# Between the experts and the next feed-forward: projecting the unnormalised sum

## The reference

```python
# end of first_block: a mixture of 16 experts is added, then a norm
x = x + scatter_add(ye)                       # the sum, 256 x 1024
x = rmsnorm(x, g_final)                       # x * rsqrt(mean(x*x) + 1e-6) * g_final
# start of second_block, for l in 0, 1:
x = x + 0.5 * swiglu(rms_norm(x, norm_ffn1[l]), ffn1_wi[l], ffn1_wo[l])
# swiglu: gate, up = split(x @ w_in); (silu(gate) * up) @ w_out,  w_in 1024 x 5632, w_out 2816 x 1024
```

## Time and profile before

| | us |
|---|---|
| median of three runs | 2795.94 |
| lowest and highest of them | 2792.14, 2796.29 |
| the profiled execution | 2791.85 |
| its span, first to last instruction | 2789.7 |
| first matmul of the first dense slot after the experts | 1437.53 |

### The profile page before, as it was taken

The page is one execution under the profiler, slowest core; times in us unless marked ns, Lnnn a source line. Parts: engine busy times, 40 slices in busy tenths (PEclk is TensorE's granted clock), DMA queues, the critical chain, the costliest instruction groups (busy, mean ns, idle before and its releaser), DMA issues.

```text
span 2789.7 us, 43821 instructions
## 1 busy us (share of the span) xinstructions
PE 2397.6 (86%) x18612; PEld 1867.8 (67%) x18612; DVE 1169.5 (42%) x1679; ACT 840.4 (30%) x1196; POOL 112.7 (4%) x107
## 2 busy tenths in 40 slices
PE   6899988778777877777779997889999999698999
PEld 6896485333333333322259996789999999488999
DVE  6757552100000000000045567566556556755655
ACT  3384121100000000000034444344445444434543
POOL 0000012000000000000010001000001000200000
PEclk9999998887887888888889997899999999699999
DMA  6435047999999999999965541143555554022553
GB/s 226 147 126 175 16 192 281 424 425 426 425 425 425 424 425 425 425 426 425 425 256 187 184 163 61 37 147 123 184 187 195 182 182 159 1 93 97 177 185 117
DMA packets 118618, 669.80 MB, mean 240 GB/s; under 512 B 10682, under 2 KB 12901, under 8 KB 60992
## 3 DMA queue, kind: packets, MB, share of 16 engines
q1 hardware_dynamic: 113376, 650.14, 59.7%
q0 software_dynamic: 2784, 13.21, 1.4%
q10 hardware_dynamic: 2304, 4.20, 0.4%
HBM read 662.26 MB, written 5.24 MB: 239 GB/s over the span
## 4 chain that ended last, share of the span: by engine, by line
PE 54%; DMA 19%; DVE 8%; SPq 7%; issue 3%; ACT 3%; DVEq 3%; POOLq 1%; POOL 0%; ACTq 0%; PEldq 0%; PEld 0%
PE psd L565 29%; PE psx L565 8%; DMA ring<-in_w_up 8%; SPq L2429 7%; DMA ring<-in_w_down 3%; DMA hx<-in_w_down 3%; PE psd L825 3%; DVE w_lo L1642 2%; DMA e_w_lo<-in_w_gate 2%; DMA ring<-in_w_gate 2%; PE psd L816 2%; DVE scr L1642 1%; PE psx L867 1%; PE psx L1062 1%; PE psd L853 1%
## 5 line engine op out<-in xcount | busy, mean ns | idle before, releaser
L565 PE MATMUL psd<-h_hi,w_hi 128*128 128x256 f32 x2448 | 703.2, 287 | 35.0 <-DVE h_lo L1642 12.8
L1642 DVE TENSOR_TENSOR w_lo<-ring,w_hi 128x1024 fp32r<-128x1024 f32 x436 | 524.2, 1243 | 434.7 <-ACT w_hi L1266 432.1
L565 PE MATMUL psd<-h_lo,w_hi 128*128 128x256 f32 x2448 | 697.0, 285 | 0.0
L565 PE MATMUL psd<-h_hi,w_lo 128*128 128x256 f32 x2448 | 696.5, 285 | 0.0
L1266 ACT ACTIVATE w_hi<-ring 128x1024 fp32r<-128x1024 f32 x436 | 435.8, 1047 | 301.6 <-PE psd L565 296.5
L565 PEld LDWEIGHTS psd<-h_hi,w_hi 128*128 128x128 f32 x2448 | 474.1, 194 | 40.9 <-issue 30.8
L565 PEld LDWEIGHTS psd<-h_lo,w_hi 128*128 128x128 f32 x2448 | 474.3, 194 | 0.3
L565 PEld LDWEIGHTS psd<-h_hi,w_lo 128*128 128x128 f32 x2448 | 474.2, 194 | 0.0
L565 PE MATMUL psx<-halves,w_hi 128*128 128x256 f32 x1408 | 255.6, 283 | 3.2 <-issue 3.2
L1642 DVE TENSOR_TENSOR scr<-psd,scr 128x512 f32<-128x512 f32 x20 | 13.8, 691 | 505.2 <-PE psd L825 505.2
L565 PEld LDWEIGHTS psx<-halves,w_hi 128*128 128x128 f32 x1408 | 219.5, 192 | 3.9 <-issue 3.9
(11 more groups left out here) (342 smaller groups left out, 2797.8 us busy)
## 6 DMA issues: line engine op xcount, KB each, us to landing
ring<-in_ffn_wi SPq DMA_DIRECT2D x88, 1024.0 KB, 4.8
scr<-in_w_gate SPq DMA_DIRECT2D x48, 1024.0 KB, 19.7
scr<-in_w_down SPq DMA_DIRECT2D x48, 1024.0 KB, 22.4
scr<-in_w_up SPq DMA_DIRECT2D x48, 1024.0 KB, 27.0
ring<-in_ffn_wo SPq DMA_DIRECT2D x44, 1024.0 KB, 4.9
ring<-in_w_gate SPq DMA_DIRECT2D x32, 1024.0 KB, 19.0
ring<-in_w_up SPq DMA_DIRECT2D x32, 1024.0 KB, 27.0
ring<-in_w_down SPq DMA_DIRECT2D x32, 1024.0 KB, 22.9
```

The source lines that it names most:

```text
L565: mm = pe.matmul(o, w[u], a[v], start=start and i == 0, stop=stop and i == 2, **kw)
L1642: return dve.tensor_tensor(o, a, b, op)
```

## The change

`g_final` and the weight of `norm_ffn10` are multiplied once at the start (`seam_gain`). After the experts both halves of the activations are made from the four PSUM banks times `seam_gain`, without either norm's root. TensorE signals each bank as its last matmul is made. The squares are of the sum times `seam_weight` = sqrt(g_final * g_final + 1e-6), and their mean plus 1e-12 is the square of the product of both norms' roots. So one root serves the projections' results. The normalised residual x is still needed: ACT squares the copied x once more, and GpSimd, TensorE and ACT take `g_final`'s own root during feed-forward steps 0 and 1. DVE inverts it in step 2 and scales two tiles of `x` in each of the steps 3 to 6. TensorE's sum for the second norm moves behind up 0. The last pair of experts is written out instead of looped, and in its second expert the cuts of the slot gate 0 are placed ahead of the wait for the expert's last matmul, on both ACT and DVE.

```diff
@@ small_plan
-    add("act", "norm", "g_final")
     for l in range(LAYERS):
         add("act", "norm", f"norm_ffn1{l}")
+        if l == 0:
+            add("act", "norm", "g_final")
@@ TensorE, ffn
+                        after_moe = (which, l) == ("ffn1", 0)
                         dense((which, l, "gate", f), g=f"norm_{which}{l}" if f == 0 else None)
-                        if f == 0:
+                        if f == 0 and not after_moe:
                             norm(f"norm_{which}{l}")
+                        if f == 1 and after_moe:
+                            norm("g_final")
                         dense((which, l, "up", f))
+                        if f == 0 and after_moe:
+                            norm(f"norm_{which}{l}")
@@ TensorE, expert and after
                 for k in range(KD):
-                    pe.matmul(acc[k // 2][:, k % 2, :], ye[...], PT, ...)
+                    mm = pe.matmul(acc[k // 2][:, k % 2, :], ye[...], PT, ...)
+                    if k % 2:
+                        mm.then_inc(S("moe_sum"), 1)
...
             pe.drain().then_inc(x_done, 4)
-            norm("g_final")
@@ ScalarE, ffn
                     act.activation(sg[:, f % 2, :, :], sg[:, f % 2, :, :], ACT.Silu).then_inc(S("silu"), 1)
+                    if (which, l, f) == ("ffn1", 0, 1):
+                        b = x_ready(act, "norm", "g_final")
+                        read(act.activation(final_rs, b[:, 0:T], ACT.Sqrt, bias=eps_col, scale=1.0 / D))
@@ ScalarE, expert
                     copy(kv_st, psd[0][:, :]).then_inc(S("kv_read"), 1)
+                    if meanwhile:
+                        meanwhile()
                     act.wait_ge(slots_done, PAIR * pair + first + ESLOTS)
                     copy(ye[:, 0, :], psd[2][:, :]).then_inc(S("ye_ready"), 1)
@@ ScalarE, after the experts
+            expert(7, 0, False)
+            expert(7, 1, False, lambda: cutter.upto(slot_of(dense0)))
+            def from_moe():
+                for i in range(4):
+                    act.wait_ge(S("moe_sum"), 4 * (EXPERTS - 1) + i + 1)
+                    for m in range(2):
+                        k = 2 * i + m
+                        ins = act.activation(h_hi[:, k, :], banks[i][:, m, :], ACT.Copy, scale=seam_gain[:, k:k + 1])
+                    ins.then_inc(S("act_hi_cut"), 1)
+                prime(cutter, dense0)
+                for i in range(4):
+                    act.wait_ge(h_ready, q + i + 1)
+                    for m in range(2):
+                        ... late_sq[k] = Square(banks[i][:, m, :] * seam_weight[k]) ...
+                    ins.then_inc(sq_ready, 1)
+                for i in range(4):
+                    XB.was_read(act, ("moe_acc", i))
+                    act.activation(sq[:, two, :], x[:, two, :], ACT.Square).then_inc(S("final_sq"), 1)
+                b = x_ready(act, "norm", "norm_ffn10")
+                read(act.activation(rstd[:, :], b[:, 0:T], ACT.Sqrt, bias=seam_eps, scale=1.0 / D))
@@ VectorE, after the experts
-            for i in range(4):
-                b = m2(x_ready(dve, "moe_acc", i))
-                read(dve.tensor_copy(x[:, 2 * i:2 * i + 2, :], b))
-            norm("g_final", x, halves_=None)
+            expert(7, 1, False, lambda: cutter.upto(slot_of(dense0)))
+            def from_moe():
+                for i in range(4):
+                    dve.wait_ge(S("act_hi_cut"), pieces[0])
+                    for m in range(2):
+                        ... h_lo[k] = banks[i][:, m, :] * seam_gain[k] - h_hi[k] ...
+                    ins.then_inc(h_ready, 1)
+                prime(cutter, dense0)
+                for i in range(4):
+                    dve.wait_ge(sq_ready, q + i + 1)
+                    read(dve.tensor_copy(x[:, 2 * i:2 * i + 2, :], banks[i]))
+                XB.was_read(dve, ("norm", "norm_ffn10"))
+                dve.reciprocal(rstd[:, :], rstd[:, :])
@@ VectorE, ffn
+                    if (which, l) == ("ffn1", 0):
+                        if f == 2:
+                            XB.was_read(dve, ("norm", "g_final"))
+                            dve.reciprocal(final_rs, final_rs)
+                        for k in (2 * f - 6, 2 * f - 5):
+                            if 0 <= k < KD:
+                                ... x[k] = x[k] * g_final[k] * final_rs ...
@@ VectorE, at the start
+            tt_(seam_gain, g_final, g_ffn10, ALU.mult)
+            dve.memset(seam_eps, EPS * EPS)
+            tt_(seam_weight, g_final, g_final, ALU.mult)
+            dve.drain().then_inc(S("gain_squared"), 1)
@@ GpSimd
                 sum_squares(f"norm_ffn1{l}")
+                if l == 0:
+                    sum_squares("g_final")
```

More of the change, by code:

```diff
@@ L353, in program @@
         tiny = sb("tiny", [P, 64])
+        seam = sb("seam", [P, 17])
         v_first = sb("v_first", [P, HP, T])
@@ L458, in tri @@
             return bank[:, 0:HP * n].rearrange("p (q n) -> p q n", q=HP)
-        NORMS = ["g_mix", "g_ffn", "g_final"]
+        NORMS = ["g_mix", "g_ffn"]
         for l in range(LAYERS):
@@ L537, in program @@
         SUMMED = [g for g in NORMS if g in squares_of]
+        SUMMED.insert(1, "g_final")
+        seam_gain, seam_weight, seam_eps = seam[:, 0:8], seam[:, 8:16], seam[:, 16:17]
+        final_rs = at(24, T)
         squares_summed = S("squares_summed")
@@ L1292, in norm @@
                 src = x if src is None else src
-                if q and part != "g_final":
+                if q:
                     act.wait_ge(h_ready, 4 * q)
@@ L1427, in _ @@
             read(act.activation(rmem, b[:, 0:T], ACT.Sqrt, bias=eps_col, scale=1.0 / D))
+            act.wait_ge(S("gain_squared"), 1)
+            act.activation(seam_weight, seam_weight, ACT.Sqrt, bias=eps_col)
             act.wait_ge(S("lg_shift"), 1)
@@ L1436, in _, with expert @@
             act.drain().then_inc(S("kv_stage_free"), 16)
-            def expert(pair, e, keys):
+            def expert(pair, e, keys, meanwhile=None):
                     first = MOE + e * ESLOTS
@@ L1460, in expert @@
                                   kv_st).then_inc(S("kv_stage_free"), 16)
+            dense0 = ("ffn1", 0, "gate", 0)
             for keys in (True, False):
-                with act.Fori(0 if keys else 4, 4 if keys else 8) as pair:
+                with act.Fori(0 if keys else 4, 4 if keys else 7) as pair:
                     for e in range(2):
                         expert(pair, e, keys)
-            norm("g_final", "moe_acc", hi=None)
+            expert(7, 0, False)
+            expert(7, 1, False, lambda: cutter.upto(slot_of(dense0)))
@@ new lines, in from_moe @@
+            def from_moe():
+                q = 4 * NORMS.index("norm_ffn10")
+                banks = [m2(XB.bank(("moe_acc", i))) for i in range(4)]
+                for i in range(4):
+                    act.wait_ge(S("moe_sum"), 4 * (EXPERTS - 1) + i + 1)
+                    pieces[0] += 1
+                    ffn_pieces[0] += 1
+                    for m in range(2):
[6 more added lines that the diff above has]
+                    for m in range(2):
+                        k = 2 * i + m
+                        ins = act.activation(late_sq[:, k, :], banks[i][:, m, :], ACT.Square,
+                                             scale=seam_weight[:, k:k + 1])
+                    ins.then_inc(sq_ready, 1)
+                for i in range(4):
+                    XB.was_read(act, ("moe_acc", i))
+                    two = slice(2 * i, 2 * i + 2)
+                    act.activation(sq[:, two, :], x[:, two, :], ACT.Square).then_inc(S("final_sq"), 1)
+                b = x_ready(act, "norm", "norm_ffn10")
+                read(act.activation(rstd[:, :], b[:, 0:T], ACT.Sqrt, bias=seam_eps, scale=1.0 / D))
@@ L1468, in _ @@
             for l in range(LAYERS):
-                first = ("ffn1", l, "gate", 0)
-                cutter.upto(slot_of(first))
-                late_norm(f"norm_ffn1{l}", "ffn2" if l else "g_final", l - 1 if l else None, first)
                 if l == 0:
+                    from_moe()
                     act.wait_ge(S("kv_stage_free"), 16 + 16 * EXPERTS)
+                else:
+                    first = ("ffn1", l, "gate", 0)
+                    cutter.upto(slot_of(first))
+                    late_norm(f"norm_ffn1{l}", "ffn2", l - 1, first)
@@ L2008, in expert @@
                     dve.drain().then_inc(S("k_scaled"), 1)
+            dense0 = ("ffn1", 0, "gate", 0)
             for keys in (True, False):
-                with dve.Fori(0 if keys else 4, 4 if keys else 8) as pair:
+                with dve.Fori(0 if keys else 4, 4 if keys else 7) as pair:
                     for e in range(2):
                         expert(pair, e, keys)
-            for i in range(4):
-                b = m2(x_ready(dve, "moe_acc", i))
-                read(dve.tensor_copy(x[:, 2 * i:2 * i + 2, :], b))
-            norm("g_final", x, halves_=None)
+            expert(7, 0, False)
```

(26 more changed lines are left out.)

14 lines of the change are left out of this document (7 added, 7 removed).

## The result

The changed kernel is slower: ratio 1.0017, 95% interval 1.0010 to 1.0023, medians of twenty runs each 2798.9 against 2793.07 us. By the ratio that is 4.7 us more. I had forecast 5.3 us less.

What follows compares the result with a forecast made beforehand. Transfers were taken to bound up to the landing, TensorE from 1447.09. Between them, 4.7 + 3.7 + 2.3 + 0.15 + 11.5 + 1.03 + 3.76 + 0.4 + 14.7 = 42.2 against 47.5: 5.3 us less, median 2790.6, range 2783 to 2796.

Steps and rivals of the forecast that it cites:

- up to the landing the kernel is bound by the transfers: Experts, until the last `w_down` slot lands at 1414.77: transfers at 428 to 431 GB/s bind, TensorE waits between slots.
- What costs nothing: Small start operations, written-out last pair, and steps 2 to 6 add no time; uncovered, the steps' operations cost 5.3 us.
- my slower rival: L867 to the sum: the clock stays low because gate 0's feed leaves holes; 8.7 us slower, 2804.6, chance 0.05.
- The copies come late: After the last expert matmul: copies to `ye` queue behind gate 0's cuts, so L867 starts at 1421.5, 3.8 us late.
- The clock: After TensorE's 4.7 us idle gap before L867: the granted clock falls, losing 1.5 to 2.95 us, taken as 2.3.
- L867 to gate 1: L867 takes 3.72 us, 6.0 with the clock; gate 0 starts 1427.7, up 0 1433.4, sum 1439.2, squares ready in time.
- The wait behind the sum: Between L575 and gate 1: root, reciprocal and cut are no longer hidden; 3.76 us, plus 0.4 for GpSimd.
- Gate 1 to down 0: Down 0 waits for ACT's root for `g_final`, 14.7 us after gate 1's start, at 1459.1; second clock loss costs nothing more.
- the rival with a drain behind it: ACT's table switch before the `g_final` root costs 1.38 us of drain besides its load; 3.9 us less, 2792.0, chance 0.08.
- Sum of the seam: Last expert matmul to feed-forward's down 0: 42.2 us against 47.5, so 5.3 us less.
- The whole: Whole kernel: 5.3 us less, own range 2.5 to 8 less, including 1 to 2 us for later gaps meeting the clock.

## Why the prediction was wrong, point by point

- **The step that failed** is the opening one, that "up to the landing the kernel is bound by the transfers" with nothing done to them, and its echo under "What costs nothing", "Writing out the last pair: the transfers bind there". I read the binding resource as a cover under which edits are free. It is the reverse for whatever touches that resource. The sum lacks a term: the new tensor's 96 bytes ahead of twelve buffers, 8.8 us in the profile, about 10 in the runs with padding alone. It turned a gain into a loss. No rival covered it, and my slower rival was about the clock.
- **The copies come late**: right. L867 was forecast 4.7 us after the last expert matmul and came 4.64 after; gate 0's landing 0.4 after, and it was 0.37. The run with the cuts behind shows cause and price: 5.2 us with the clock's share.
- **The clock**: it fell in both gaps. L867 took 6.75 us instead of the 6.0 forecast, so the loss was 3.0 us, the upper bound, not 2.3. That size is chance: with the same gap of 4.65 us the same matmuls took 6.39 with `seam` last and 5.13 with 64 words, a loss of 2.7 and 1.4. That the clock would still be at 0.5 in gate 0 was wrong; it was back at 1.0. In the run without the first gap it stayed up until the second.
- **L867 to gate 1**: gate 0 11.6 us after the last expert matmul, forecast 10.9. The feed from PSUM kept up: TensorE was busy throughout 1440.6 to 1453. The sum waited for nothing.
- **The wait behind the sum**: 3.7 us, forecast 3.76, and 0.4 more for GpSimd in the way of the cut. The 0.4 was not there; GpSimd had been done for 2.7 us. ACT's eight squares took 3.03 us instead of 3.6, and GpSimd's six operations 1.28 to 1.31 each, where I took 1.44 to 1.80.
- **Gate 1 to down 0**: 14.6 us, forecast 14.7, and released by ACT's root with 0.6 us of waiting. ACT's table load ended 0.02 us before that root, so the switch cost its 1.28 us alone, and the rival with a drain behind it falls.
- **Sum of the seam**: 42.6 us, forecast 42.2. That it comes so near is in part luck: 0.7 more up to gate 0 by the clock, 0.4 less for GpSimd. The gain of 5.3 was reckoned against this one trace of the kernel before, which has the longest seam of eight; against their mean it is 4.4.
- **The whole**: with the addresses mended the kernel came to 0.9987 and 0.9988, that is 3.6 and 3.4 us less. The forecast 5.3 lies in both intervals, but so do gains of little more than 1 us, and the kernel before with 64 words gained as much. The 2 to 3 us that all changed kernels lose in the second layer are a second thing that the sum lacks; it has 1 to 2 us for later gaps in its range only.

## What to carry to other kernels

Where transfers set the time, look at what a diff does to the tensors' start addresses before anything else: one small tensor in the middle of a layout cost about twice what the reordered seam gained. Before a gain of a few us is credited to a change, compare with the old kernel at the same addresses: here the old kernel at other addresses, with the same transfer rate, measured 0.1% less. Put small tensors last or round them to 256 bytes, and check the rate in the windows of a stage that the change doesn't touch. Work that is only "moved ahead of a wait" needs its own inputs' landing checked against what stands behind it on the same engine.

## What the runs showed of the hardware that I had not expected

- Transfers of 1 MB slots into SBUF ran at 425 GB/s where the destinations started at multiples of 256 bytes in the partition, and at 421 where twelve of sixteen started at other addresses, namely odd multiples of 32, 64 or 128 bytes. With all sixteen at odd multiples of 64 it was 418:

```profile
500.00:1380.00 880.00, 657.67 (x3895) 284.87 (x3887) 54.47 (x102) 61.98 (x87) 0.00 (x0) 0.82 1.02 418
```

- TensorE's rate for the same matmuls depended on where its operands lie relative to each other. With the weights and the activations a multiple of 256 bytes apart (49152 or 49408), 48 float32 matmuls of 256 columns took 5.76 us; with 49216 bytes 5.66 and with 49344 bytes 5.46, a gain of 5%. The reason, and whether gate and up slots could have it too, wasn't tried.
